# Hybrid attention and state-space trunk: top-k rounds moved between the steps of the attention loop, and six kinds of elementwise work from VectorE to GpSimd

## The reference

```python
proj = h @ w_in
q, k, v, qi, ki, wi, u = jnp.split(proj, IN_SPLITS, axis=-1)
q, k, qi, ki = rope(q), rope(k), rope(qi), rope(ki)       # first 16 of 64 features rotated
# attention, in blocks of 128 queries
rel = relu(einsum('bqhd,bsd->bqhs', qib, ki))
score = einsum('bqhs,bqh->bqs', rel, wb) * idx_scale       # keys of later chunks: -inf
vals, idx = lax.top_k(score, 128)                          # 128 keys for each query
p = softmax(q . k[idx] * att_scale);  attn = p @ v[idx]    # 8 heads, one key/value head
# state-space branch
y = gelu(s5_ssm(u));  y = y * sigmoid(y @ glu_w + glu_b)
mixed = concat([rms_norm(attn), rms_norm(y)]) @ w_out
```

## Time and profile before

| | us |
|---|---|
| median of 3 runs | 2104.31 |
| lowest and highest | 2103.47, 2107.48 |
| the profiled execution, its time | 2102.22 |
| its span in the profile | 2100.4 |
| TensorE matmuls busy | 2023.8 (96%) |
| VectorE busy | 1317.9 (63%) |
| ScalarE busy | 693.9 (33%) |
| GpSimd busy | 260.1 (12%) |

### The profile page before, as it was taken

One profiled execution on the slowest core, in us unless ns is written; L12 is line 12 of the kernel. 1 busy time (PEld: TensorE's weight loads), 2 busy tenths in 40 slices (PEclk: granted clock), 3 DMA queues, 4 the chain that ended last, 5 costly groups with the idle time before them and its releaser, 6 DMA issues.

```text
span 2100.4 us, 25289 instructions
## 1 busy us (share of the span) xinstructions
PE 2023.8 (96%) x9548; PEld 1632.4 (78%) x9548; DVE 1317.9 (63%) x2057; ACT 693.9 (33%) x1061; POOL 260.1 (12%) x231
## 2 busy tenths in 40 slices
PE   6999899999899999999999999999998999999998
PEld 5788678877577788888878877888775787888886
DVE  6778856566884764543467697375779656545334
ACT  4332222341444422222342322233334534223223
POOL 0006900400100000000000295040001000000000
PEclk8999999999799999999999999999997999999999
DMA  8465556343101454433347365444320135463332
GB/s 290 124 212 186 157 155 183 86 109 94 56 20 52 135 172 145 158 103 92 89 139 222 121 185 152 152 146 112 100 70 22 41 89 172 120 193 115 104 93 78
DMA packets 395985, 264.77 MB, mean 126 GB/s; under 512 B 56560, under 2 KB 371672, under 8 KB 395864
## 3 DMA queue, kind: packets, MB, share of 16 engines
q1 hardware_dynamic: 387360, 260.94, 41.1%
q10 hardware_dynamic: 8504, 2.22, 0.5%
HBM read 254.98 MB, written 6.29 MB: 124 GB/s over the span
## 4 chain that ended last, share of the span: by engine, by line
PE 65%; issue 21%; DVE 9%; ACT 3%; DMA 1%; SPq 0%; POOL 0%; ACTq 0%; DVEq 0%; POOLq 0%
PE ps L1706 19%; PE ps L1707 18%; PE ps L1708 18%; DVE w_lo L1003 2%; DVE mod_acc L1024 2%; PE ps L1990 2%; PE ps L2009 1%; DVE h_lo L1084 1%; PE ps L1934 1%; PE ps L2017 1%; PE ps L2000 1%; PE ps L2082 1%; DMA stage<-in_ffn_w 1%; PE ps L2087 1%; PE ps L1970 1%
## 5 line engine op out<-in xcount | busy, mean ns | idle before, releaser
L1706 PE MATMUL ps<-h_hi,w_hi 128*128 128x512 f32 x1728 | 686.0, 397 | 22.1 <-DVE w_lo L1003 19.3
L1707 PE MATMUL ps<-h_lo,w_hi 128*128 128x512 f32 x1728 | 677.7, 392 | 0.0
L1708 PE MATMUL ps<-h_hi,w_lo 128*128 128x512 f32 x1728 | 677.1, 392 | 0.0
L1003 DVE TENSOR_TENSOR w_lo<-stage,w_hi 128x1024 fp32r<-128x1024 f32 (+2 forms) x322 | 394.1, 1246 | 164.4 <-ACT w_hi L698 162.1
L1706 PEld LDWEIGHTS ps<-h_hi,w_hi 128*128 128x128 f32 x1728 | 327.1, 189 | 103.7 <-DVE w_lo L1003 21.9
L1708 PEld LDWEIGHTS ps<-h_hi,w_lo 128*128 128x128 f32 x1728 | 327.1, 189 | 69.7
L1707 PEld LDWEIGHTS ps<-h_lo,w_hi 128*128 128x128 f32 x1728 | 327.0, 189 | 65.5 <-issue 0.5
L698 ACT ACTIVATE w_hi<-stage 128x1024 fp32r<-128x1024 f32 (+2 forms) x322 | 318.9, 1016 | 172.3 <-PE ps L1708 165.1
L1706 PE MATMUL ps<-g_hi,w_hi 128*128 128x512 f32 x704 | 276.7, 393 | 1.1 <-DVE g_lo L1318 1.1
L1707 PE MATMUL ps<-g_lo,w_hi 128*128 128x512 f32 x704 | 274.2, 389 | 0.0
L1708 PE MATMUL ps<-g_hi,w_lo 128*128 128x512 f32 x704 | 274.2, 389 | 0.0
(11 more groups left out here) (304 smaller groups left out, 1790.6 us busy)
## 6 DMA issues: line engine op xcount, KB each, us to landing
stage<-in_ffn_w SPq DMA_DIRECT2D x210, 512.0 KB, 4.7
mod_stage<-in_mod_w SPq DMA_DIRECT2D x144, 512.0 KB, 5.6
stage<-in_ffn_w SPq DMA_DIRECT2D x64, 448.0 KB, 4.0
stage<-in_w_in SPq DMA_DIRECT2D x20, 512.0 KB, 3.8
mod_first<-in_mod_w SPq DMA_DIRECT2D x16, 512.0 KB, 9.4
stage<-in_w_out SPq DMA_DIRECT2D x16, 512.0 KB, 4.1
x_in<-in_x SPq DMA_DIRECT2D x4, 512.0 KB, 5.1
stage<-in_w_in SPq DMA_DIRECT2D x8, 256.0 KB, 3.7
```

Of the source, the lines that this page charges most:

```text
L1003: V.tensor_tensor(w_lo[:, c % RING, 0:n], stage[:, c % RING, 0:n], w_hi[:, c % RING, 0:n].bitcast(F32), ALU.subtract).then_inc(w_split_lo. ...
L1706: mm(out, hi, rhs_hi, start=first, stop=False)
L1707: mm(out, hi, rhs_lo, start=False, stop=False)
L1708: return mm(out, lo, rhs_hi, start=False, stop=last)
```

## The change

It leaves the computation as it is and changes who does what, and when:

- Three of block 1's rounds go from steps 5 to 7 into tile 11, which then has five. Three of block 3's rounds go from steps 13 to 15 into steps 16 to 18, each behind that step's own round.
- Rotation 6 is divided as rotation 7 was: VectorE makes the product with the sine, GpSimd the product with the cosine and the sum. Its parts lie in `tmp_b`, which the exponentials also use, so ScalarE waits for the rotation ahead of step 0.
- The low parts of chunks 14 and 15, the four gates (one VectorE instruction each, two on GpSimd), and the low parts of the attention output of blocks 0 and 1 go to GpSimd.

```diff
-GATE_AT = {13 + 2 * n: n for n in range(ST)}
-TOPK_WITH = [(1, 2)] * HEADS + [(2, 3)] * HEADS + [(3,)] * HEADS + [()] * HEADS
+TOPK_WITH = [(1, 2)] * 5 + [(2,)] * 3 + [(2, 3)] * 5 + [(2,)] * 3 + [(3,)] * HEADS + [()] * HEADS
+TOPK_MORE = (16, 17, 18)
...
                 act.wait_ge(*h_done.at(l, 2 * KT - 1))
+                act.wait_ge(*rope_done.at(l, 6))
...
+                def rope_sin(r):
+
+                    dve.wait_ge(*swap_mm.at(l, r))
+                    if r == 7:
+                        dve.wait_ge(*rope_done.at(l, 6))
+                    V.tensor_tensor((tmp_b if r == 6 else ssm_t)[:, 1, :], ps[:, ROPE_BANKS[r][1], :], rope_s[:], ALU.mult).then_inc(last_sin.sem, 1)
...
-                    if i == 8:
+                    if i == 8 and b >= 2:
                         dve.wait_ge(*att_hi.at(l, b))
+                        if b == 2:
+                            dve.wait_ge(*att_done.at(l, 1))
...
-                        for _ in range(2):
+                        for _ in range(2 if t == 10 else 5):
                             topk_max(1)
                             topk_take(1)
                     for r in ROPE_SLOT.get(t, ()):
-                        rope(r)
+                        (rope if r < 6 else rope_sin)(r)
...
-                    if blocks and h == HEADS - 1:
-                        topk_end(blocks[0])
+                    if e in TOPK_MORE:
+                        topk_max(3)
+                        topk_take(3)
+                    if h == HEADS - 1 and b + 1 < QB:
+                        topk_end(b + 1)
                     if e == LAST_ROPE:
-                        dve.wait_ge(*swap_mm.at(l, 7))
-                        V.tensor_tensor(ssm_t[:, 1, :], ps[:, ROPE_BANKS[7][1], :], rope_s[:], ALU.mult).then_inc(last_sin.sem, 1)
-                    if e in GATE_AT:
-                        n = GATE_AT[e]
-                        dve.wait_ge(*glu_act.at(l, n))
-                        V.scalar_tensor_tensor(out=ssm_t[:, n, :], in0=glu_t[:, n % 2, :], scalar=1.0,
-                                               in1=u_t[:, n].rearrange("p a b -> p (a b)"), op0=ALU.add, op1=ALU.mult).then_inc(ssm_y.sem, 1)
-                    if e - 1 in OUT_SPLIT_AT:
+                        rope_sin(7)
+                    if e - 1 in OUT_SPLIT_AT and e > 2:
+                        dve.wait_ge(*w_split_lo.at(l, m0 + OUT_SPLIT_AT[e - 1] - 1))
                         split_lo(l, m0 + OUT_SPLIT_AT[e - 1])
...
+            def w_low(l, c):
+
+                n = chunk_size(c)
+                pool.wait_ge(*w_split_hi.at(l, c))
+                pool.wait_ge(*w_split_lo.at(l, c - 1))
+                Q.tensor_tensor(w_lo[:, c % RING, 0:n], stage[:, c % RING, 0:n],
+                                w_hi[:, c % RING, 0:n].bitcast(F32), ALU.subtract).then_inc(w_split_lo.sem, 1)
+
+            def att_low(l, b):
+
+                pool.wait_ge(*att_hi.at(l, b))
+                Q.tensor_tensor(h_lo[:, 0:AT, b * P:(b + 1) * P], z_t[:, 1, :].rearrange("p (m t) -> p m t", m=AT),
+                                h_hi[:, 0:AT, b * P:(b + 1) * P].bitcast(F32), ALU.subtract).then_inc(att_done.sem, 1)
+
+            def gate_y(l, n):
+
+                y = u_t[:, n].rearrange("p a b -> p (a b)")
+                pool.wait_ge(*glu_act.at(l, n))
+                Q.tensor_tensor(glu_t[:, n % 2, :], glu_t[:, n % 2, :], y, ALU.mult).then_inc(pool_half.sem, 1)
+                pool.wait_ge(*pool_half.at(l, 2 + n))
+                Q.tensor_tensor(ssm_t[:, n, :], glu_t[:, n % 2, :], y, ALU.add).then_inc(ssm_y.sem, 1)
+
+            def rope_add(l, r):
+
+                pool.wait_ge(*z_copy.at(l, ROPE_TILE[r]))
+                pool.wait_ge(*rope_done.at(l, r - 1))
+                part = tmp_b if r == 6 else ssm_t
+                Q.tensor_tensor(part[:, 0, :], z_t[:, ROPE_TILE[r] % 2, :], rope_c[:], ALU.mult).then_inc(pool_half.sem, 1)
+                pool.wait_ge(*pool_half.at(l, r - 6))
+                pool.wait_ge(*last_sin.at(l, r - 6))
+                Q.tensor_tensor(q_t[:, r - 4, :], part[:, 0, :], part[:, 1, :], ALU.add).then_inc(rope_done.sem, 1)
...
                 power(l, 1)
+                rope_add(l, 6)
                 for m in range(ST):
                     y_low(l, m)
-                last_rope(l)
-                for b in range(2):
-                    att_power(b)
+                rope_add(l, 7)
+                for n in range(2):
+                    w_low(l, MIX_BASE + 14 + n)
+                att_power(0)
+                gate_y(l, 0)
+                gate_y(l, 1)
+                att_low(l, 0)
+                gate_y(l, 2)
+                att_power(1)
+                gate_y(l, 3)
                 power(l, 2)
+                att_low(l, 1)
```

More of the change, by code:

```diff
@@ L122 @@
         PREP[4 * m + i + 1] = (m, i)
-DVE_STEPS, POOL_STEPS = 273, 86
+DVE_STEPS, POOL_STEPS = 271, 86
 SMALL = 72
@@ L378, in trunk @@
         rope_done = Signal(sem("rope_done"), 8)
-        last_sin = Signal(sem("last_sin"), 1)
-        last_cos = Signal(sem("last_cos"), 1)
+        last_sin = Signal(sem("last_sin"), 2)
+        pool_half = Signal(sem("pool_half"), ST + 2)
         v_tr = Signal(sem("v_tr"), 1)
```

## The result

The change made the kernel very slightly slower: median 2107.46 us over 20 runs (2102.90 to 2111.72) against 2103.89 over 20 runs of the kernel before (2101.63 to 2107.74). The ratio is 1.0017, with a 95% interval of 1.001 to 1.0024: +3.6 us, from 2.1 to 5.0. So the difference is clear of zero, but smaller than the spread of either kernel's own executions. The profiled execution took 2107.37 us, with a span of 2105.6.

What follows compares the result with a forecast made beforehand. TensorE's pace was taken to bound the kernel, VectorE counting only where it holds TensorE up, last at step 9. +0.6 and +0.4 a layer made +2.0 over two layers: median 2106.3 us, range 2102.5 to 2110.5.

Steps and rivals of the forecast that it cites:

- Three rounds of 1.20 in tile 11: Before step 0: three more serial rounds add 3.60 us, rotation 6's departed work takes off 1.57; first mask 2.03 later.
- the collision: GpSimd's cosine product of rotation 6 slows VectorE's score accumulation beside it: 0.4 us a layer, bounds 0 and 0.6.
- The table load behind both waits: ScalarE ahead of step 0: the exponential's table load follows the new wait for rotation 6, starting 2.94 us later.
- The sine of rotation 7 set by the swap product: Step 3: VectorE arrives first and waits for TensorE's swap product, so sine and logits 6 come 1.7 us later.
- The start of step 8's value products: Last point where VectorE moves TensorE, in step 9: 0.6 us later, plus 0.4 for the collision.
- Steps 10 to 15 at price zero: Three rounds (3.6 us) and gates (1.2) leave VectorE there, but TensorE sets the pace, so nothing is gained.
- rival A: VectorE paces through step 15: 7.0 us a layer faster, 2090; or steps 0 to 9 only, 2101.3; chance 0.05.
- Steps 16 to 19 at price zero: Block 3's three extra rounds, 5.1 us in all, fit with a margin of about 0.8 before step 19's transpose.
- Rival B: Extra rounds overrun in steps 16 to 19: up to 4.3 + 1.0 a layer, 2115, halfway 2111; chance 0.14.
- Gate 3: On GpSimd, done near 613.5, its square 1.3 us later, step 20's copy 0.5; the transpose behind has over a us.
- rival D: GpSimd's new list is late for square 3 or step 24: under 1 us a layer, 2107 to 2108; chance 0.12.
- Rival C: The loop's entry costs nothing: GpSimd's sum and the table load overlap, no collision; 2104, no change; chance 0.14.

Runs made afterwards that it cites:

- e4: The changed kernel with the four gates and the low parts of attention blocks 0 and 1 back on VectorE; 1.0083 of the kernel before.
- e5: The changed kernel with the exponential's table loaded early by a one-column exponential, `small` made one column wider for it; 2116.56 us, 1.0057 of the kernel before.
- f1: The changed kernel with the table loaded early, the one-column exponential written to a free column of `small`, nothing widened; 2103.76 us, 1.0005 of the kernel before.
- e3: The changed kernel with GpSimd's cosine product of rotation 6 held back until the last score accumulation is done; 0.9999 of the kernel before.
- f4: f2 with block 3's rounds back in steps 13 to 15 too, so no round is moved; 2096.77 us, 0.9973 of the kernel before.
- f2: The changed kernel with block 1's rounds back, cosine product held back and table loaded early, `small` not widened; 2095.52 us, 0.9968 of the kernel before.
- e1: The changed kernel with block 1's three rounds back in steps 5 to 7; 1.0003 of the kernel before.
- e2: The changed kernel with three more rounds in tile 11, eight instead of five, taken from steps 2 to 4; 1.0056 of the kernel before.
- e8: The changed kernel with the edits of e1, e3 and e5 together, `small` one column wider; 1.003 of the kernel before.
- e7: The changed kernel with all six top-k rounds back, only the moves to GpSimd kept; 0.9996 of the kernel before.
- f3: The kernel before with `small` one column (4 bytes a partition) wider and nothing else; 1.0067 of the kernel before.
- e6: The kernel before with only the six top-k rounds moved, nothing to GpSimd; 2119.94 us, 1.0075 of the kernel before.

## Why the prediction was right, and where it was off

**The class and the sum.** Predicted 2106.3, +2.0 and not to be told from no change; measured 2107.46, +3.6. Twenty runs of each do tell it from no change (2.1 to 5.0). In the loops, +1.0 a layer was forecast and +1.21 and +1.30 came. That the loops come so near is partly luck: behind att_n(0) the slow matmuls, which the sum doesn't have, happened to be about as many as before (5 and 6). With the twelve of e4's layer 0, which starts alike, the loop would have been 2.4 longer.

**Three rounds of 1.20 in tile 11: right.** They start 1.20 to 1.21 apart. Mask 0 moved by 2.71, where 2.03 and the collision's 0.4 made 2.43.

**The table load behind both waits: right.** ScalarE's idle time ends with q_t, and the load follows. +3.59, where 2.94 + 0.4 = 3.34 was forecast. e5 and f1 show its price by the other side: loading earlier gains 1.28. The Trainium skill (ScalarE: Activation LUTs, "What ACT_TABLE_LOAD costs") gives 1.28 us for the load and about as much again for a drain; the load agrees, but the exponential starts 1.30 after the load begins (560.81, 562.11), and hiding it gained no more than 1.28, so no drain shows here.

**The sine of rotation 7 set by the swap product: right, but only just.** The product ends at 570.39 and the sine starts at 570.43; VectorE's instruction ahead of it ended at 570.29, 0.1 earlier, where the forecast had 0.4. Logits 6 moved by 2.32 (1.7 + 0.4 = 2.1).

**The start of step 8's value products: +1.44, not +1.0.** e3 splits it: 0.74 of entry (predicted 0.6) and 0.70 of collision (predicted 0.4). **The collision is the mis-sized term.** I took it by the low part at 559.28, which lost 0.37. The row after shows 1.43 against 0.74, and 0.85 of waiting behind it on ScalarE against 0.16. The cosine product ends at 547.98, 0.55 before the accumulation does, which fits the accumulation doing most of its 0.73 only afterwards. The Trainium skill (SBUF — State Buffer, "Who interferes with whom") has it so, an exclusive lock; by that the price was my upper bound of 0.6, which lies nearer to the measured 0.69 than my 0.4 did. The 0.69 lies beyond the bound because the product itself took 1.50 instead of the 1.3 that I had laid out (from the first logits, its end came at -6.09 instead of -6.35).

**Steps 10 to 15 at price zero: right**, and so rival A fell: the 3.6 + 1.2 that left VectorE there came back nowhere, and of the 2.2 that left steps 5 to 7 at most 0.9 did (from +2.31 at logits 8 to +1.44). f4 against f2 says it again for block 3's rounds.

**Steps 16 to 19 at price zero: right, with a margin of 0.4 instead of 0.8, and not for the reason given.** Exponential 19 ends at 614.60, its transpose starts at 614.98. The forecast counted on VectorE entering step 16 early. But it sits idle for TensorE's value products ahead of mask 18, as the timeline of VectorE in the kernel after shows:

```profile
606.50 0.20 DVE L1433 RECIPROCAL small<-small 128x8 f32<-128x8 f32 x1 [0.77 <-PE ps L2050]
```

In e4 the same instruction waits for nothing (608.12), which is late. What VectorE saved before that point is gone with its wait there, and the margin is 0.37 to 0.38 in both layers of every version with the extra rounds and the gates on GpSimd (after, e1, e2, e3, e5, e8, f1, f2), however early or late its loop is. Without the extra rounds (before, e7, f3, f4) it is 0.55. Rival B's mechanism is real all the same: without the gates' move (e4, e6) it comes, and at more than the lateness. Its price was reckoned in VectorE's time; the larger part of what followed it in e4's and e6's layer 0 is TensorE's clock.

**Gate 3 (rival D): harmless, as said.** Its second part ends at 618.10, and the next wait of TensorE is one of 0.67 at 645.70, which the kernel before has too. **Rival C** fell with the +1.44. f1, in which the load does run under the wait, comes nearest to it (+0.15), though it still has the collision.

**Not foreseen at all**: that what is gained or lost before step 10 doesn't simply carry through. The number of slow matmuls behind it, 6 or 12, decides over 2.4 us a layer (75.2 us or 77.9 from att_n(0) to the loop's end, e2's layers 1 and 0). In e3, f1, f2 and f4 the loop's end moves by what att_n(0) moved, to within 0.6 us; in e1 and e7 it does not.

**Open.** What makes it 6 or 12: starting 1.2 us earlier gave 12, 3.1 earlier gave 6, and the same +1.4 gave 5 in the kernel after and 12 in e4. It wasn't settled. Neither was why e4's two equal waits had unequal sequels. And of the +3.6, 1.1 isn't in the two profiled loops, and e1's loops are as long and its ratio lower. So the loops of one execution don't add up to the medians. The kernel after also spreads more (2102.9 to 2111.7) than e3 (2101.8 to 2104.2). Within its executions the time goes with the mean granted clock: 0.979 in the four fastest (up to 2104.19), 0.975 or 0.976 in the three slowest (from 2111.06). Where in the kernel the slow ones lose it no trace shows; the margin of step 19 is no likely place, since e3 has the same.

## What to carry to other kernels

Where an engine is idle only behind a serial chain, that chain's entry is the one place where its time counts in full: three rounds put there cost 3.6 us a layer, of which 2.6 were left when TensorE's own pace took over; block 3's three rounds, taken out of steps at TensorE's pace, gave nothing. Before putting a new wait on an engine, look what it holds up that doesn't need it, here a table load (1.28 us) that a one-column activation ahead of the wait takes away. And run an unrelated 4-byte change of the layout as a control before blaming an edit that moves tensors: it was worth 14 us here, more than the whole study's subject.

## What the runs showed of the hardware

- A float32r matmul with 512 streamed columns took 389 ns and, with its streamed tensor 4 bytes further on, 395 (f3, on g; the first of a set 393 and 399).
- A table load stood behind the semaphore waits of the exponential that needed it (560.81, after 6.89 idle) and took 1.28 us. With a one-column exponential ahead of those waits the load ran before them, in ScalarE's idle time, and exp 0 came 1.28 earlier (e5, f1).
- A VectorE accumulation with two SBUF inputs took 1.43 us beside a GpSimd product, 0.73 to 0.74 without. Beside the gate of 616.63, a 1024-wide low part took 2.14.
- TensorE's granted clock was 0.56 and 0.58 in the window of ten us behind a wait of 0.54 and 0.53 (e4, e6, layer 0), 0.83 behind one of 0.54 in e6's layer 1, and 1.00 behind the same wait in e4's layer 1. The Trainium skill (TensorE: Matmul & The Clock Gate, "HAM oscillation — how this bites in real kernels") tells of a kernel in which repeated DMA waits of some us take the clock down. The waits here are single and far shorter, so these rows neither confirm nor refute it, and no run here isolates the wait as the cause.
